# Two transformer blocks on one core: an opening in another order, squares added before TensorE sums them, and sixteen gate vectors moved from the queries' stage to the early experts

## The chip, the cores and the metric

The kernel runs on 1 core of one Trainium2 chip, in a single launch. Its time is the device time of that launch, in microseconds (us). The time of the kernel before is the median of 3 runs.

## What is computed

Two blocks over T = 256 tokens of width D = 2048, in fp32. The first has a forgetting attention beside a gated linear recurrence, and a PEER layer of 16384 experts; the second an S5 state-space mixer with a gated linear unit and a native sparse attention. What matters here, of the first block:

```python
mod = sc @ w_ada[l] + b_ada[l]                      # sc = silu(c)
sh1, sc1, ga1, sh2, sc2, ga2 = jnp.split(mod, N_ADA, axis=-1)
h = _rmsnorm(x, g_mix[l]) * (1.0 + sc1[:, None, :]) + sh1[:, None, :]
mix = _hybrid_mixer(h, w_in[l], ...)                # ends in merged @ w_out
x = x + ga1[:, None, :] * mix
h = _rmsnorm(x, g_ffn[l]) * (1.0 + sc2[:, None, :]) + sh2[:, None, :]
x = x + ga2[:, None, :] * _peer(h, peer_w_q[l], peer_k1[l], peer_k2[l], peer_u[l], peer_v[l])
```

`_peer` projects queries, takes the top 16 of 128 keys twice, combines them, takes the top 16 again and a softmax, and sums the chosen experts' rows of `peer_v`, each weighted by the softmax and by gelu(peer_u row . h). The second block has vectors of the same kind from `w_mod2` and a second condition `c2`.

## The kernel before, in words

It is a hand-written program of five instruction streams: TensorE (PE), VectorE (DVE), ScalarE (ACT), GpSimd (POOL) and SyncE (SP). Named semaphores tie them, and `meet` is a barrier of all of them. Activations stand transposed, 128 features on the partitions and 256 tokens beside, so D is KT = 16 chunks.

**Weights** come in tiles of 1 MB (128x2048 fp32) into `ring`, which has four slots. SP issues their loads in the written order (`load`, L407): tile `pos` waits until slot `pos % 4` is free, so a slot returned late holds up every later load on that queue. `STAGES` gives each stage's tiles for one pass of its loop, the passes, and how many of the tiles are for TensorE and how many are vectors. The stages run in this order: shift_scale, heads, w_out, topk (the PEER queries), tail, hots, early, peer, turn, ssm, glu, ssm_out, kv, nsa, w_o.

**Vectors.** One chunk of a modulation vector is the row sums of a tile of `w_ada` or `w_mod2` times `cond` = silu(c), in two halves. `whole_vec` (L1486 to L1490) does it on DVE in two custom operations and returns the tile's slot. In topk another pair does it for the chunks 80 to 95, which gate the PEER output and aren't read before its end: POOL multiplies the tile by `cond` in place (`vec_times`, L2203), ACT sums it (`vec_sum`). `take_mod` moves finished sums into `mod`.

**Opening.** SP loads four modulation tiles, x, and then tiles and three first `w_in` tiles by turns; ACT's queue loads `cond`, then `vec` (gains and biases). DVE makes 32 vectors, works out the norm's factor rstd once six pairs are done (`norm_rstd`), and writes the normed rows of H as pairs of vectors become ready (L1578). TensorE makes the three first products of head 0 from `head_vec`, chunk by chunk with H. Beside each head's eight ring tiles, three vector tiles go into `head_vec` (`head_beside`) and DVE sums them at L1636.

**Norms.** ACT squares x in pieces (`PIECES`: chunks 0-4, 4-8, 8-12, 12-15, 15-16), and TensorE sums the 16 square tiles with a matrix of ones: `norm_sums` (L600), and `merged_sums` (L608) for two norms over half the width each.

**topk and tail.** Each of 8 heads is two query products (`gemm`, L520), eight score matmuls of the head before (L748) around half a hidden product, and that product's other half. DVE copies the scores (L1739) and picks the best keys; the equality tests against `iota_t` are at L1760. Tail is eight more hidden products, five of them before the transposes of the picked (L763), then `meet`, then three. **Hots** goes on with 16 products; beside them TensorE spreads the weights over a dense block (L780) and ACT copies that (`copy_tokens`). `early_hidden` stores gelu values.

**Early experts.** 32 tiles of peer_v in four groups g of eight tiles j, in two halves. ACT makes a tile's high half `vhi` (L1228), DVE the rest `vlo` (L1804), TensorE multiplies them by the weights' own parts Ghi and Glo (L583, L584, L590) into four banks, and DVE adds each bank to the rows y (`add_rows`, L1812) one group later, at even j. POOL clears y (L2216, `y_clear`). DVE makes the weights of the next group between (`early_weigh`, `early_low`; L1818, L1823). **peer** runs the remaining experts in the same manner, with its own vector tiles (`vbuf`).

## Time and profile before

| | us |
|---|---|
| Median of 3 runs | 3670.26 (3666.49 to 3670.36) |
| The profiled execution | 3664.94 |
| Its span, first to last instruction | 3663.2 |
| Mean granted clock of TensorE | 0.975 |

The span lies 1.7 us under the profiled execution's own time. Times in the trace count from the span's start. On every row the first number is the start, the second the duration; a group of equal instructions is one row with their count, and its duration runs from the first start to the last end, so matmuls that overlap are counted once. What stands in square brackets is the engine's idle time before the row, and what ended it.

### The profile page before, as it was taken

To read this page: it belongs to the slowest core of one execution; us is meant where nothing else is said; L and a number is where in the kernel's file an instruction comes from. 1 tells how busy PE (TensorE), PEld (TensorE's weight loads), DVE (VectorE), ACT (ScalarE), POOL (GpSimd) and SP (SyncE) were. 2 spreads that over 40 slices of the span, in tenths; PEclk is the share of its full clock that TensorE was granted. 3 is DMA by queue.
4 is the path that set the end of the run, shared out by engine and by line. 5 is a ranking of instruction groups with operands and counts; after the bars stand their busy time and mean duration, and the time that the engine had idled before them with its cause. 6 is when DMAs were issued, how large, how long until landed. Compare 5 with 4: busy or idle time off the path is not lost. (4 is left out here: it accounts for less than half of the span.)

```text
span 3663.2 us, 56553 instructions
## 1 busy us (share of the span) xinstructions
PE 3460.7 (94%) x20712; PEld 3063.9 (84%) x20712; DVE 2454.7 (67%) x4494; ACT 1339.0 (37%) x2000; POOL 387.9 (11%) x405
## 2 busy tenths in 40 slices
PE   3799998889989999999999999899999899999998
PEld 2688887779977999999999998577779898999998
DVE  7666556877367777777777776888834634666664
ACT  1232312212234444444444444211112434555553
POOL 0000113410000000000000000577710000000000
PEclk7899998989999999999999999899999999999999
DMA  9678744555765888888888886122246643555543
GB/s 394 267 297 304 257 167 182 202 179 201 263 234 207 297 296 298 295 296 300 298 288 295 297 296 234 58 92 92 92 151 228 247 150 130 188 188 186 184 173 127
DMA packets 123316, 817.72 MB, mean 223 GB/s; under 512 B 12848, under 2 KB 18224, under 8 KB 27184
## 3 DMA queue, kind: packets, MB, share of 16 engines
q1 hardware_dynamic: 105552, 760.26, 57.4%
q10 hardware_dynamic: 17632, 55.63, 4.0%
q8 instruction: 91, 1.49, 0.2%
q14 instruction: 41, 0.34, 0.0%
HBM read 791.65 MB, written 24.18 MB: 223 GB/s over the span
## 5 line engine op out<-in xcount | busy, mean ns | idle before, releaser
L520 PE MATMUL bank<-H,ring 128*128 128x256 f32 x3744 | 849.4, 386 | 39.6 <-ACT H L1064 17.5
L520 PEld LDWEIGHTS bank<-H,ring 128*128 128x128 f32 x3744 | 715.4, 193 | 161.3 <-issue 58.2
L1804 DVE TENSOR_TENSOR vlo<-ring,vhi 128x1024 fp32r<-128x1024 f32 x448 | 548.2, 1225 | 308.1 <-ACT vhi L1228 294.5
L1228 ACT ACTIVATE vhi<-ring 128x1024 fp32r<-128x1024 f32 x448 | 474.8, 1060 | 627.8 <-PE bank L590 350.0
L556 PE MATMUL bank<-Hhi,whi 128*128 128x256 f32 x1920 | 484.0, 290 | 21.1 <-DVE Hlo L1511 10.2
L1500 DVE TENSOR_TENSOR wlo<-ring,whi 128x1024 fp32r<-128x1024 f32 x240 | 292.8, 1227 | 308.3 <-ACT whi L1035 305.1
L557 PE MATMUL bank<-Hlo,whi 128*128 128x256 f32 x1920 | 474.2, 285 | 0.0
L584 PE MATMUL bank<-vhi,Glo 128*128 128x512 f32 x1024 | 400.6, 391 | 0.0
L583 PE MATMUL bank<-vhi,Ghi 128*128 128x512 f32 x1024 | 400.6, 391 | 0.0
L556 PEld LDWEIGHTS bank<-Hhi,whi 128*128 128x128 f32 x1920 | 370.3, 193 | 31.5 <-issue 17.7
L535 PE MATMUL bank<-Fhi,vhi 128*128 128x256 f32 x1536 | 373.0, 280 | 0.0
L536 PE MATMUL bank<-Flo,vhi 128*128 128x256 f32 x1536 | 372.9, 283 | 0.0
L557 PEld LDWEIGHTS bank<-Hlo,whi 128*128 128x128 f32 x1920 | 371.4, 193 | 0.0
L1035 ACT ACTIVATE whi<-ring 128x1024 fp32r<-128x1024 f32 x240 | 253.9, 1059 | 312.3 <-PE bank L561 294.1
L536 PEld LDWEIGHTS bank<-Flo,vhi 128*128 128x128 f32 x1536 | 290.4, 189 | 0.5
L535 PEld LDWEIGHTS bank<-Fhi,vhi 128*128 128x128 f32 x1536 | 288.5, 188 | 0.5
L590 PE MATMUL bank<-vlo,Ghi 128*128 128x512 f32 x1024 | 276.5, 392 | 12.7 <-DVE vlo L1804 12.7
L561 PE MATMUL bank<-Hhi,wlo 128*128 128x256 f32 x1920 | 271.3, 285 | 0.0
L561 PEld LDWEIGHTS bank<-Hhi,wlo 128*128 128x128 f32 x1920 | 249.8, 194 | 0.0
L590 PEld LDWEIGHTS bank<-vlo,Ghi 128*128 128x128 f32 x1024 | 192.3, 188 | 56.1 <-DVE vlo L1804 16.0
L1881 DVE CUSTOM_DVE_ANT_0 arena<-arena,cond 128x1024 f32<-128x1024 f32 x192 | 234.0, 1219 | 0.0
L583 PEld LDWEIGHTS bank<-vhi,Ghi 128*128 128x128 f32 x1024 | 192.7, 188 | 41.4 <-issue 0.9
(412 smaller groups left out, 4489.1 us busy)
## 6 DMA issues: line engine op xcount, KB each, us to landing
ring<-in_peer_u SPq DMA_DIRECT2D x128, 1024.0 KB, 5.5
ring<-in_peer_v SPq DMA_DIRECT2D x128, 1024.0 KB, 5.1
arena<-in_w_mod SPq DMA_DIRECT2D x96, 1024.0 KB, 7.3
ring<-in_w_ada SPq DMA_DIRECT2D x72, 1024.0 KB, 6.4
ring<-in_w_qz SPq DMA_DIRECT2D x64, 1024.0 KB, 4.8
ring<-in_w_in SPq DMA_DIRECT2D x37, 1024.0 KB, 6.0
ring<-in_w_mod SPq DMA_DIRECT2D x32, 1024.0 KB, 5.0
ring<-in_ssm_in SPq DMA_DIRECT2D x32, 1024.0 KB, 5.1
```

The costliest lines, as they stand in the source:

```text
L520: last = mm(out, ring[:, pos % R, k, :], rhs[:, k, :], start=(k == 0), stop=(k == KT - 1))
L535: mm(out, u_hi[:, k, :], Fhi[:, kk, :], start=(kk == 0), stop=False)
L536: mm(out, u_hi[:, k, :], Flo[:, kk, :], start=False, stop=False)
L556: mm(out, whi[:, half, k, :], Hhi[:, kk, :], start=(kk == 0), stop=False)
L557: mm(out, whi[:, half, k, :], Hlo[:, kk, :], start=False, stop=False)
L561: last = mm(out, wlo[:, half, k, :], Hhi[:, kk, :], start=False, stop=(kk == KT - 1))
L583: mm(pair[th][:], G_hi[part][:, n, tok], vhi[:, half, k, :], start=(n == 0), stop=False)
L584: mm(pair[th][:], G_lo[part][:, n, tok], vhi[:, half, k, :], start=False, stop=False)
L590: last = mm(pair[th][:], G_hi[part][:, n, tok], vlo[:, half, k, :], start=False, stop=(n == 7))
L1228: A(vhi[:, half], v_half(pos, half), ACT.Copy).then_inc(s("vhi_ready"), 1)
L1500: v.tensor_tensor(wlo[:, half], ring[:, pos % R, 8 * half:8 * half + 8, :], whi[:, half].bitcast(F32), ALU.subtract).then_inc(s("wlo_ready ...
L1804: v.tensor_tensor(vlo[:, half], v_half(pos, half), vhi[:, half].bitcast(F32), ALU.subtract)\
```

## The change

- **Opening.** `cond` is the first load on SP's queue; eight modulation tiles stand before x; five first `w_in` tiles in place of three, in `scratch`; TensorE reads two more of head 0's products from there. DVE waits for `vec` only at m == 7, where the norm's factor and the first rows stand too. The three loads beside head 0 come after the wait for `f_in_psum`, behind all of head 0's tiles, and DVE's sums of them after the attention's probabilities.
- **Norms' squares.** POOL adds square tiles in pairs (`add_squares`, and a loop of 12 adds for the merged norms); TensorE sums 6 tiles in place of 16, and 4 in place of 16 for the merged. The final norm of the first block stays as it was.
- **Gate vectors.** The tiles 80 to 95 of `w_ada` leave topk, whose loop has 12 tiles in place of 20, and go to early, four in each group, on DVE. Early's four `w_mod2` tiles move into peer's numbering, and four of peer's go to glu, which has 8 vectors in place of 4. The load and Silu of the second condition move from behind the tail to early's last group.
- **Tail and hots.** Seven tail products stand before the transposes and one after the barrier. In hots the product comes before the spread on TensorE, and `early_hidden` before `copy_tokens` on ACT.
- **y.** DVE's wait for the clearing of y moves from before the early loop to before the first `add_rows`.

```diff
-STAGES = dict(shift_scale=(4, 8, 4, 2), heads=(8, HEADS, 5, 3), w_out=(8, 2, 8, 0), topk=(20, 2, 12, 0),
-              tail=(8, 1, 8, 0), hots=(16, 1, 16, 0), early=(36, 1, 32, 4), peer=(16, 12, 16, 0),
-              ssm=(4, 8, 4, 0), glu=(20, 1, 16, 4), ssm_out=(24, 1, 16, 8), kv=(8, 3, 8, 0),
+STAGES = dict(shift_scale=(4, 8, 4, 2), heads=(8, HEADS, 5, 3), w_out=(8, 2, 8, 0), topk=(12, 2, 12, 0),
+              tail=(8, 1, 8, 0), hots=(16, 1, 16, 0), early=(48, 1, 32, 16), peer=(16, 12, 16, 0),
+              ssm=(4, 8, 4, 0), glu=(24, 1, 16, 8), ssm_out=(24, 1, 16, 8), kv=(8, 3, 8, 0),
...
+EARLY_VEC = [(0, 2, 4, 6)] * 3 + [(0, 1, 2, 3)]
...
-            if k == 3:
-                out.append(("w_mod2", g))
+            if k in EARLY_VEC[g]:
+                out.append(("w_ada", 80 + 4 * g + EARLY_VEC[g].index(k)))
...
-GLU_M = [4, 9, 14, 19]
-GLU_W = [pos for pos in range(20) if pos not in GLU_M]
+GLU_M = list(range(2, 24, 3))
+GLU_W = [pos for pos in range(24) if pos not in GLU_M]
...
-FIRST = (0, 1, 4)
+FIRST = (0, 1, 4, 3, 6)
...
-        first_w = head_vec[:].rearrange("p n (k m) -> p n k m", k=KT)
+        first_w = scratch[:, 0:5 * D].rearrange("p (n k m) -> p n k m", n=5, k=KT)
...
+            def first_load(n):
+                sp.dma_start(first_w[:, n], a["w_in"][HEAD_W.index(FIRST[n])]).then_inc(first_loaded[max(n - 2, 0)], 16)
...
+            sp.dma_start(cond[:], a["c"].broadcast_to([P, D])).then_inc(s("cond_loaded"), 16)
             mod_tiles(0, first=True)
+            mod_tiles(1)
             sp.dma_start(x[:], a["x"]).then_inc(x_loaded, 16)
-            for n, pos in enumerate(FIRST):
-                mod_tiles(n + 1)
-                sp.dma_start(first_w[:, n], a["w_in"][HEAD_W.index(pos)]).then_inc(first_loaded[n], 16)
-            with sp.Fori(4, 8) as i:
+            for n in range(4):
+                mod_tiles(n + 2)
+                first_load(n)
+            with sp.Fori(6, 8) as i:
                 mod_tiles(i)
+            first_load(4)
             sp.dma_start(gate_w, a["gate_w"][0]).then_inc(s("gatew_loaded"), 16)
...
-                if pos == 2:
-                    sp.wait_ge(s("f_in_psum"), 1)
-                if pos in (2, 5, 7):
-                    head_beside(0, HEAD_M.index(pos))
+            sp.wait_ge(s("f_in_psum"), 1)
+            for n in range(3):
+                head_beside(0, n)
...
-                        load("topk", i, 5 * h + k, a["w_q"][8 * i + 2 * h + k])
-                    for k in range(2):
-                        load("topk", i, 5 * h + 2 + k, a["w_ada"][80 + 8 * i + 2 * h + k])
-                    load("topk", i, 5 * h + 4, a["peer_u"][4 * i + h])
+                        load("topk", i, 3 * h + k, a["w_q"][8 * i + 2 * h + k])
+                    load("topk", i, 3 * h + 2, a["peer_u"][4 * i + h])
...
-                        sp.dma_start(vbuf[:, n % 2], a["w_mod2"][4 + 8 * i + n].rearrange("p k n -> p (k n)"))\
+                        sp.dma_start(vbuf[:, n % 2], a["w_mod2"][8 * i + n].rearrange("p k n -> p (k n)"))\
...
+            def added_sums(n, name):
+                pe.wait_ge(s("squares_added"), n + 2)
+                for t in range(2):
+                    mm(WA[:, 0:T], ones[:, 0:P], SQ[:, t, :], start=(t == 0), stop=False)
+                for p in (3, 4):
+                    pe.wait_ge(s("squares_ready"), SQUARES[name] + p + 1)
+                    for t in range(*PIECES[p]):
+                        last = mm(WA[:, 0:T], ones[:, 0:P], SQ[:, t, :], start=False, stop=(t == KT - 1))
+                last.then_inc(s("sums_ready"), 1)
...
-                for h in range(HEADS):
-                    for g in range(2):
-                        pe.wait_ge(s("squares_ready"), SQUARES["merged"] + 2 * h + g + 1)
-                        last = mm((WA, WB)[g][:, 0:T], ones[:, 0:P], SQ[:, HEADS * g + h, :], start=(h == 0), stop=(h == HEADS - 1))
+                pe.wait_ge(s("squares_added"), 1)
+                for g in range(2):
+                    mm((WA, WB)[g][:, 0:T], ones[:, 0:P], SQ[:, HEADS * g, :], start=True, stop=False)
+                for g in range(2):
+                    pe.wait_ge(s("squares_ready"), SQUARES["merged"] + 2 * (HEADS - 1) + g + 1)
+                    last = mm((WA, WB)[g][:, 0:T], ones[:, 0:P], SQ[:, HEADS * g + HEADS - 1, :], start=False, stop=True)
...
-            for n, b in enumerate((2, 0, 1)):
+            for b in (2, 0, 1):
                 pe.wait_ge(bank_free[b], 1)
-                pe.wait_ge(first_loaded[n], 16)
+            pe.wait_ge(first_loaded[0], 48)
...
-            gemm("heads", 0, 3, banks[0][:, T:2 * T], 0)
+            def first_product(n, out, lo, hi):
+                for k in range(lo, hi):
+                    last = mm(out, first_w[:, n, k, :], H[:, k, :], start=(k == 0), stop=(k == KT - 1))
+                return last
+            pe.wait_ge(first_loaded[1], 16)
+            first_product(3, banks[0][:, T:2 * T], 0, KT).then_inc(slot_free[3], 1)
             head_gates(0)
-            gemm("heads", 0, 6, banks[3][:, 0:T], 3, 0, halves=(0,))
+            pe.wait_ge(bank_free[3], 1)
+            pe.wait_ge(first_loaded[2], 16)
+            first_product(4, banks[3][:, 0:T], 0, 8)
             head_scores(0)
-            gemm("heads", 0, 6, banks[3][:, 0:T], 3, halves=(1,))
+            pe.wait_ge(slot_free[2], use_of("heads", 0, 6))
+            first_product(4, banks[3][:, 0:T], 8, KT).then_inc(slot_free[2], 1)
...
-            norm_sums("ffn")
+            added_sums(0, "ffn")
...
-                    gemm("topk", i, 5 * h + 4, banks[b][:, 0:T], b, uses[b] + 2 * i + h // 2, halves=(0,))
+                    gemm("topk", i, 3 * h + 2, banks[b][:, 0:T], b, uses[b] + 2 * i + h // 2, halves=(0,))
...
-            for pos in range(5):
+            for pos in range(7):
...
-            for pos in range(5, 8):
-                tail(pos)
+            tail(7)
...
+                gemm("hots", 0, c, banks[c % 4][:, 0:T], c % 4, uses[c % 4] + c // 4)
                 for u in range(3 * c, min(3 * c + 3, 32)):
                     spread_tokens(u)
-                gemm("hots", 0, c, banks[c % 4][:, 0:T], c % 4, uses[c % 4] + c // 4)
...
-            def vec_sum(i, pos, n, col, half):
-                act.wait_ge(s("prod_ready"), 2 * (8 * i + n) + half + 1)
-                w = ring[:, pos % R, 8 * half:8 * half + 8, :].rearrange("p k n -> p (k n)")
-                A(w, w, ACT.Copy, accum_out=mod_ab[:, half, bass.ds(col, 1)])
-                if half == 1:
-                    act.drain().then_inc(slot_free[pos % R], 1)
...
-            act.dma_start(cond[:], a["c"].broadcast_to([P, D])).then_inc(s("cond_loaded"), 16)
...
-                    for k in range(2):
-                        for half in range(2):
-                            vec_sum(i, 5 * h + 2 + k, 2 * h + k, 80 + 8 * i + 2 * h + k, half)
...
+            for pos in range(5, 7):
+                early_hidden("tail", 0, pos, 8 + pos, pos % 4, 2 + pos // 4, pos % 4)
...
-            act.dma_start(cond[:], a["c2"].broadcast_to([P, D])).then_inc(s("cond_loaded"), 16)
             act.sem_inc(s("spread_copied"), 3)
-            act.wait_ge(s("cond_loaded"), 32)
-            A(cond[:], cond[:], ACT.Silu).then_inc(s("cond_ready"), 1)
-            for pos in range(5, 8):
-                early_hidden("tail", 0, pos, 8 + pos, pos % 4, 2 + pos // 4, pos % 4)
+            early_hidden("tail", 0, 7, 15, 3, 3, 3)
...
-                for m in range(6 * c, min(6 * c + 6, 64)):
-                    copy_tokens(m)
...
+                for m in range(6 * c, min(6 * c + 6, 64)):
+                    copy_tokens(m)
...
+                    if g == 3 and j == 5:
+                        product(act, "early", 0, AT["early", "w_ada", 95])
+                        act.dma_start(cond[:], a["c2"].broadcast_to([P, D])).then_inc(s("cond_loaded"), 16)
+                    if g == 3 and j == 7:
+                        act.wait_ge(s("cond_loaded"), 32)
+                        A(cond[:], cond[:], ACT.Silu).then_inc(s("cond_ready"), 1)
...
-            dve.wait_ge(vec_in, 16)
             for m in range(KT):
                 for k in range(2):
                     whole_vec("shift_scale", m // 2, 2 * (m % 2) + k, m + KT * k)
-                if m == 5:
+                if m == 7:
+                    dve.wait_ge(vec_in, 16)
                     norm_rstd("mix", D)
...
-            with dve.Fori(0, HEADS) as i:
+            def vectors(i):
...
+            def head(i, first=False):
...
+                if not first:
+                    vectors(i)
...
+                if first:
+                    vectors(i)
...
+            head(0, first=True)
+            with dve.Fori(1, HEADS) as i:
+                head(i)
...
-            take_mod(80, 96)
-            dve.wait_ge(s("cond_ready"), 2)
...
-            dve.wait_ge(s("y_clear"), 1)
...
+                        if g == 0 and j == 2:
+                            dve.wait_ge(s("y_clear"), 1)
                         add_rows(16 * g, j // 2 - 1)
-                    if j == 4:
-                        whole_vec("early", 0, AT["early", "w_mod2", g], 96 + g)
+                    if j - 1 in EARLY_VEC[g]:
+                        n = 80 + 4 * g + EARLY_VEC[g].index(j - 1)
+                        whole_vec("early", 0, AT["early", "w_ada", n], n)
...
+            take_mod(80, 96)
...
+            dve.wait_ge(s("cond_ready"), 2)
...
-                v.tensor_copy(mod_ab[:, :, bass.ds(100 + 8 * i, 8)], peer_sums)
+                v.tensor_copy(mod_ab[:, :, bass.ds(96 + 8 * i, 8)], peer_sums)
...
-                if g % 4 == 3:
-                    whole_vec("glu", 0, GLU_M[g // 4], 196 + g // 4)
+                if g % 2 == 1:
+                    whole_vec("glu", 0, GLU_M[g // 2], 192 + g // 2)
...
+            for i in range(1, HEADS - 1):
+                for g in range(2):
+                    pool.wait_ge(s("squares_ready"), SQUARES["merged"] + 2 * i + g + 1)
+                    tt(SQ[:, HEADS * g, :], SQ[:, HEADS * g, :], SQ[:, HEADS * g + i, :], ALU.add)
+                pool.drain()
+            pool.drain().then_inc(s("squares_added"), 1)
+            def add_squares(name):
+                for p in range(3):
+                    pool.wait_ge(s("squares_ready"), SQUARES[name] + p + 1)
+                    tt(SQ[:, 4 * p:4 * p + 2, :], SQ[:, 4 * p:4 * p + 2, :], SQ[:, 4 * p + 2:4 * p + 4, :], ALU.add)
+                    pool.drain()
+                    if p:
+                        tt(SQ[:, 0:2, :], SQ[:, 0:2, :], SQ[:, 4 * p:4 * p + 2, :], ALU.add)
+                        pool.drain()
+                pool.drain().then_inc(s("squares_added"), 1)
...
+            add_squares("ffn")
...
-                w = ring[:, pos % R, 8 * half:8 * half + 8, :].rearrange("p k n -> p (k n)")
-                gp.tensor_tensor(w, w, cond[:, D // 2 * half:D // 2 * half + D // 2], ALU.mult)\
-                    .then_inc(s("prod_ready"), 1)
...
```

The first loads on SP's queue, before. `cond` isn't among them, since ACT's queue loads it; `head_vec` holds the first `w_in` tiles.

```order
L407 DMA ring<-in_w_ada 128x2048 x4
L434 DMA x<-in_x 128x4096
L407 DMA ring<-in_w_ada 128x2048 x4
L437 DMA head_vec<-in_w_in 128x2048
L407 DMA ring<-in_w_ada 128x2048 x4
```

And in the change:

```order
L439 DMA cond<-in_c 128x2048
L410 DMA ring<-in_w_ada 128x2048 x8
L442 DMA x<-in_x 128x4096
L410 DMA ring<-in_w_ada 128x2048 x4
L437 DMA scratch<-in_w_in 128x2048
L410 DMA ring<-in_w_ada 128x2048 x4
```

`cond` has come in front, and x stands four modulation tiles further back.

TensorE at the tail, before: the products of 16 matmuls each, the transposes of the picked (into work_a, b, c), and the first of hots.

```order
L520 MATMUL bank<-H,ring 128x256 x80
L763 MATMUL work_a<-ident,arena 128x128 x2
L763 MATMUL work_b<-ident,arena 128x128 x2
L763 MATMUL work_c<-ident,arena 128x128 x2
L520 MATMUL bank<-H,ring 128x256 x48
L780 MATMUL work_a<-hotB,hotA 128x128 x4
```

And in the change:

```order
L526 MATMUL bank<-H,ring 128x256 x112
L791 MATMUL work_a<-ident,arena 128x128 x2
L791 MATMUL work_b<-ident,arena 128x128 x2
L791 MATMUL work_c<-ident,arena 128x128 x2
L526 MATMUL bank<-H,ring 128x256 x32
L807 MATMUL work_a<-hotB,hotA 128x128 x4
```

Two products of 16 matmuls have moved ahead of the transposes; behind them stand one of the tail and the first of hots.

SP's queue in early, before:

```order
L407 DMA ring<-in_peer_u 128x2048 x24
L407 DMA ring<-in_peer_v 128x2048 x4
L407 DMA ring<-in_w_mod 128x2048
L407 DMA ring<-in_peer_v 128x2048 x8
L407 DMA ring<-in_w_mod 128x2048
L407 DMA ring<-in_peer_v 128x2048 x8
```

And in the change:

```order
L410 DMA ring<-in_peer_u 128x2048 x24
L410 DMA ring<-in_peer_v 128x2048
L410 DMA ring<-in_w_ada 128x2048
L410 DMA ring<-in_peer_v 128x2048 x2
L410 DMA ring<-in_w_ada 128x2048
L410 DMA ring<-in_peer_v 128x2048 x2
L410 DMA ring<-in_w_ada 128x2048
```

Every third tile is now a vector's, where it was every ninth; the last group has its four by turns with single peer_v tiles.

## Rows read from the trace of the kernel before

**Rows 1.** The page's line on each engine: busy us, share of the span, instructions.
```profile
PE 3460.7 (94%) x20712; PEld 3063.9 (84%) x20712; DVE 2454.7 (67%) x4494; ACT 1339.0 (37%) x2000; POOL 387.9 (11%) x405
```

**Rows 2.** TensorE's waits: engine, line, waited for: us in total, times, longest.
```profile
PE work_a L748 <- DVE arena L1739: 18.2, 4, 8.8
...
PE bank L590 <- DVE vlo L1804: 12.7, 7, 8.7
```

**Rows 3.** The opening as a window: us, PE, PEld, DVE, ACT, POOL, clock, DMA share, GB/s.
```profile
12.00:60.00 48.00, 9.36 (x33) 7.68 (x34) 41.26 (x83) 11.24 (x17) 0.00 (x0) 0.76 1.01 422
```

**Rows 4.** Timeline, opening and head 0: start, us, engine, line, operation, count [idle before <-releaser].
```profile
14.28 1.22 DVE L1486 CUSTOM_DVE_ANT_0 ring<-ring,cond 128x1024 f32<-128x1024 f32 x1 [12.92 <-DMA vec<-in_vec]
...
111.86 0.48 DVE L1578 SCALAR_TENSOR_TENSOR arena<-x,gain,rstd 128x256 f32<-128x256 f32 x1
...
122.47 8.80 PE L520 MATMUL bank<-H,ring 128*128 128x256 f32 x32 [7.18 <-DMA ring<-in_w_in]
...
139.85 1.22 DVE L1636 CUSTOM_DVE_ANT_0 head_vec<-head_vec,cond 128x1024 f32<-128x1024 f32 x1 [7.07 <-DMA head_vec<-in_w_ada]
...
150.04 22.40 PE L520 MATMUL bank<-H,ring 128*128 128x256 f32 x96
```

**Rows 5.** Timeline, TensorE, the merged norm's sums and w_out.
```profile
428.51 0.70 PE L608 MATMUL work_a<-arena,ones 128*128 128x256 f32 x2 [1.01 <-ACT arena L1129]
...
435.52 110.67 PE L726 MATMUL bank<-arena,ring 128*128 128x256 f32 x512
```

**Rows 6.** Timeline, sums of the ffn and the last norm, with their last squares.
```profile
546.02 7.07 PE L600 MATMUL work_a<-arena,ones 128*128 128x256 f32 x32
...
548.14 0.42 ACT L1046 ACTIVATE arena<-x 128x256 f32<-128x256 f32 x1 [5.98 <-DVE x L1680]
...
3642.49 7.07 PE L600 MATMUL work_a<-arena,ones 128*128 128x256 f32 x32
...
3643.21 0.42 ACT L1046 ACTIVATE arena<-x 128x256 f32<-128x256 f32 x1 [2.60 <-DVE x L2008]
```

**Rows 7.** Timeline, GpSimd and VectorE in the queries' stage.
```profile
599.08 9.48 POOL L2203 TENSOR_TENSOR ring<-ring,cond 128x1024 f32<-128x1024 f32 x4 [36.43 <-DMA ring<-in_w_ada]
...
603.93 4.91 DVE L1760 TENSOR_TENSOR arena<-arena,iota_t 128x256 f32<-128x256 f32 x2
...
765.90 0.69 DVE L1739 COPY arena<-work_a 128x512 f32<-128x512 f32 x1 [0.51 <-issue]
...
774.59 0.76 DVE L1760 TENSOR_TENSOR arena<-arena,iota_t 128x256 f32<-128x256 f32 x2
...
788.28 0.69 DVE L1739 COPY arena<-work_a 128x512 f32<-128x512 f32 x1 [0.51 <-issue]
```

**Rows 8.** Timeline, TensorE, two heads of the queries' stage and the tail.
```profile
591.70 20.89 PE L520 MATMUL bank<-H,ring 128*128 128x256 f32 x96
...
613.31 20.89 PE L520 MATMUL bank<-H,ring 128*128 128x256 f32 x96
...
813.04 0.69 PE L763 MATMUL work_a<-ident,arena 128*128 128x128 f32 x2 [7.04 <-DVEq L1784]
...
815.62 22.49 PE L520 MATMUL bank<-H,ring 128*128 128x256 f32 x96 [1.05 <-ACTq L368]
```

**Rows 9.** Timeline, early experts: y's memset, and TensorE's passes with the low halves.
```profile
1011.51 3.51 POOL L2216 MEMSET y<- 128x4096 f32 x1 [252.43 <-DMA early_hidden<-y]
...
1016.38 2.08 PE L590 MATMUL bank<-vlo,Ghi 128*128 128x512 f32 x4 [8.75 <-DVE vlo L1804]
...
1046.46 1.20 PE L590 MATMUL bank<-vlo,Ghi 128*128 128x512 f32 x4 [0.73 <-DVE vlo L1804]
...
1049.31 1.07 PE L590 MATMUL bank<-vlo,Ghi 128*128 128x512 f32 x4
...
1052.03 1.07 PE L590 MATMUL bank<-vlo,Ghi 128*128 128x512 f32 x4
```

**Rows 10.** Loads of ring tiles by SyncE from 1020 to 1070 us, summary.
```profile
DMA to landing us min/median/max: 4.7/4.8/7.7
```

More of the change, by code:

```diff
@@ L487, in _ @@
                     load("ssm", i, 2 * t + 1, a["ssm_in"][KT + 2 * i + t])
-            for pos in range(20):
-                load("glu", 0, pos, a["w_mod2"][100 + GLU_M.index(pos)] if pos in GLU_M else a["w_glu"][GLU_W.index(pos)])
+            for pos in range(24):
+                load("glu", 0, pos, a["w_mod2"][96 + GLU_M.index(pos)] if pos in GLU_M else a["w_glu"][GLU_W.index(pos)])
             for pos in range(24):
@@ L750, in _ @@
                     last.then_inc(s("s_in_psum"), 1)
-                    gemm("topk", i, 5 * h + 4, banks[b][:, 0:T], b, halves=(1,))
+                    gemm("topk", i, 3 * h + 2, banks[b][:, 0:T], b, halves=(1,))
             for b in range(4):
@@ L1011, in _ @@
                 uses[b] += 4
-            norm_sums("final2")
+            added_sums(2, "final2")
             meet(pe, met)
@@ L1615, in _ @@
             conv_w = V("conv_w").rearrange("p (a b) -> p a b", b=4)
-            with dve.Fori(0, HEADS) as i:
+            def vectors(i):
+                for n in range(3):
+                    dve.wait_ge(head_loaded[n], 16 * (i + 1))
+                    for half in range(2):
+                        w = head_vec[:, n, D // 2 * half:D // 2 * half + D // 2]
+                        ins = v.tensor_tensor_reduce(w, w, cond[:, D // 2 * half:D // 2 * half + D // 2], 1.0, 0.0,
+                                                     ALU.mult, ALU.add, accum_out=head_sums[:, half, n:n + 1])
+                    ins.then_inc(head_free[n], 1)
+                dve.drain()
+                v.tensor_copy(mod_ab[:, :, bass.ds(56 + 3 * i, 3)], head_sums[:])
+            def head(i, first=False):
                 v.tensor_scalar(cm[:, 0, :], fl[:, 5, :], ident[0:8, bass.ds(i, 1)], None, ALU.mult)
@@ L2271, in _ @@
             meet(pool, met)
+            add_squares("final2")
             meet(pool, met)
```

36 lines of the change are left out of this document (10 added, 26 removed).

## The prediction, made before the changed kernel ran

> **What bounds the kernel now.** I read the page's engine line first, then TensorE's waits, then the timeline around each place that the change touches. The engine line [rows 1]: TensorE (PE) is busy 94% of the span, VectorE (DVE) 67%. So time can only come from PE's gaps, or from work taken off PE. PE's waits [rows 2] name two gaps that the edits aim at: 18.2 us in four waits for DVE's copy of the queries' scores (L1739), and 12.7 us in seven waits for the low halves of peer_v (L1804), 8.7 of it once. The other targets are the opening, where PE has next to nothing to do, and the norms' sums. 0.2% of the time, 7.3 us, is about what this measurement tells from no change.
>
> **Opening and head 0.** In the window from 12 to 60 us [rows 3] PE is busy 9.36 of 48 us, DVE 41.26, and the DMA engines are full (share 1.01, 422 GB/s, so 1 MB takes about 2.49 us). DVE's first vector op starts at 14.28 [rows 4], after 12.92 us for `vec`. Now `cond` is first on the SP queue and the wait for `vec` moves behind vector 16: I put the start at about 8. But `cond`, 16 modulation tiles, x (2 MB) and one first tile, 20 MB, land by 3 + 20 x 2.49 = 53, so the vectors then wait for DMA, and DVE's sixteenth ends at 55 to 56, not earlier for its early start. From there DVE is the bound as before: the norm's rstd and eight rows, moved here, about 7.5; 16 tiles of some 2.6 (two 1.22 us ops [rows 4] and what reads them out), 41; the other rows, 5. The last row of H, at 111.86 before [rows 4], comes at about 110: 2 us earlier. What goes as well is head 0's wait for its weight tile (7.18) and the cold product behind it (8.80 for one of about 7) [rows 4], since its two products now sit in scratch. The loads of head 0's three vectors, on which DVE waited 7.07 to 139.85 [rows 4], move behind `f_in_psum` on the SP queue, and head 1's weights stand behind them: head 0's attention, with PE busy on nothing else, ends some 12 us earlier, at 138, while head 1's three first tiles land at about 140, 150 (its slot waits for DVE's vector) and 157. Before, head 1's product began at 150.04 [rows 4]; its third tile is then about 8 earlier than before. Bounds: 2 + 1 for the earlier row alone, and the whole 12 less one for the rest. I take 8, **-8 (-11 to -3)**.
>
> **Norms' squares.** Before, the merged norm's sums run from 428.51 to 435.52 as 16 matmuls [rows 5]. Now POOL has added heads 1 to 6 while the heads ran, and 4 matmuls of 0.44 are left: 1.8 in place of 7.0, **-5.2**. For the ffn norm, 16 matmuls take 7.07 from 546.02, to 553.09; the last square ends at 548.56 [rows 6]. With 6 matmuls the sum ends about 0.5 behind that square, 549.1: **-4.0**. For final2, 3642.49 + 7.07 = 3649.56, the last square 3643.63 [rows 6]; POOL's last add, of a piece squared earlier, and the last two matmuls end at about 3645.2: -4.4, and l1 is built alike: **-8.8** for both. POOL's adds cost about 1.2 us each (half of the 128x1024 one of 9.48 / 4 us [rows 7]), five a norm, beside PE's last products.
>
> **Queries' stage.** In the four heads with the longest waits, POOL multiplies gate vectors (9.48 us for four [rows 7]) and the DVE pair at L1760 takes 4.91; with POOL silent the same pair takes 0.76 [rows 7]. The 32 POOL ops go, so all heads should run like the undisturbed ones: DVE's copies of two such heads start at 765.90 and 788.28, 22.38 apart [rows 7]. PE's head is 613.31 - 591.70 = 21.61 long [rows 8]. The waits of 18.2 us [rows 2] go; DVE then falls 0.8 us a head behind, which PE's next scores don't notice within eight heads. On the clock of before: DVE's first copy at about 592, its eighth at 592 + 7 x 22.38 = 748.6, and the picked some 24.8 later (a head and the softmax), at 773, in place of 813.04. PE's eighth scores begin at 613.31 + 6 x 21.61 - 0.9 = 742.1; they, a half product (3.45) and seven tail products of 6.91 (a third of 20.89 [rows 8]) fill it to 794.8. The picked are there first, so the 7.04 us wait before the transposes [rows 8] goes. The transposes, copies and barrier keep 2.6 (813.04 to 815.62), the last product takes 6.9: hots begin at 804.3, before at 815.62 + 22.49 = 838.11 [rows 8]. **-33.8**: 18.2 and 7.0 are the waits, the other 8 the slower PE behind each (22.49 in place of 20.89 for 96 matmuls [rows 8], three such groups, and scores). Were only the waits worth something, it would be -25, the lower end. In the tail ACT's early_hidden has two more products before the barrier; they hide.
>
> **The wait for y's clearing.** The memset of y starts at 1011.51, released by the store of early hidden values, takes 3.51, and DVE waited for it before the first low half: PE stalls 8.75 us to 1016.38 and its next pass is cold, 2.08 for one of 1.07 [rows 9]. The wait now stands before the first add_rows, two tiles (10.9 us) later. PE starts at 1007.6, but ACT waits for the same store until 1011.5 and makes the second tile's high half only then; about 2 is given back. **-8 (-10 to -4.5)**: if the memset held DVE's lows for its 3.51 us, as POOL's multiplications held L1760, it would be -4.5. The Trainium skill (SBUF — State Buffer, Who interferes with whom) says that a DVE instruction with two SBUF inputs contends with a GpSimd instruction that reads SBUF, and not with one that only writes it, as a memset. By that rule the sum is -54.3, by L1760's rows taken over to the memset -50.8; no row here shows the two side by side.
>
> **Early experts.** 12 tiles more: 16 vectors in place of 4. A PE half takes 2.72 us (1049.31 to 1052.03 [rows 9]), a tile 5.44, its weights 4.8 from issue to landing [rows 10]. DVE has the 2.4 us for a vector in an odd tile, where it has no rows to add. But the ring has four slots, and a vector's slot goes back only behind DVE's turn in the next tile. So the peer_v tile that follows in that slot is issued late; ACT's high half is wanted about 2.5 us before PE's product, and I get 0.6 to 0.75 us of stall a vector for 12 of them (0.73 follows the vector before 1046.46 now [rows 9]), 8; the last group has four vectors in a row, 6; a group's loads by ACT beside them 2. The six stalls of before, 12.7 - 8.7 = 4.0 [rows 2], are in these: -4. **+12 (+5 to +20)**. The four shifted w_mod2 vectors in peer take the place of others, glu gets four more beside DVE idle time: 0, the cover being 5 us a pair; if it were gone, 2.6 each.
>
> **Small.** In hots the product goes before the spread, the store of early hidden values lands about 1 later; `cond`'s Silu sits beside the last early tile. **+1.5**.
>
> **Sum.** -8 - 5.2 - 4.0 - 8.8 - 33.8 - 8 + 12 + 1.5 = -54.3. From the profiled execution's 3664.94 that is 3611; it lies 5.3 below the median 3670.26, to which the sum is carried over: 3670.3 - 54.3 = 3616. I say **3615**. Bounds of the terms added as squares: (5, 9, 3.5, 8) give about 13.
>
> **Rivals.**
> - Early vectors hidden as DVE's idle time would allow (for: 1.1 us idle between lows; against: slot order above): +12 becomes 0, **3604**. 12%.
> - DVE's slow pairs aren't POOL's doing, so the queries' stage still has PE waiting (for: the overlap could be coincidence; against: 4.91 and 0.76 split exactly so). Then only tail order is left, -8.8: **3641**. 6%.
> - The opening gains nothing, since head 1's tiles come when they came (for: they queue behind the moved loads): **3623**. 6%.
> - POOL's adds read SBUF while DVE makes low halves for the last products, each side holding the other as at L1760. Five adds of about 1.2 in each of two norms, all exposed, is 12: **3628**. 5%. The Trainium skill's rule on the shared port (SBUF — State Buffer, Who interferes with whom) says that they would, this time against the change; the trace agrees in L1760's 4.91 us, but shows no POOL add beside a low.
> - The change doesn't do what it says in the tail (picked later than PE's seventh product): up to 7 lost, **3622**. 2%.
> - **Slower**: each of 16 gate tiles in early exposes its whole landing, since ring order makes each peer_v tile wait for a vector's slot. 16 x 4.8 [rows 10] = 77 in place of 12: **3681**. It decides from (54.3 + 12) / 16 = 4.1 us a vector on. For: in order ring, DVE's turn late. Against: three other slots are full, 4 us of slack. 3%.
> - The forecast as it stands: 66%.
>
> **How the numbers follow.** The predicted time is that of the forecast, 3615. Its own range is 13 either way, 3602 to 3628. The hidden case widens it to 3600; of the upper ones 3641 lies apart, and reaching to 3637 takes in the forecast's bounds with the opening's and adds' cases together. Left out: 3641 and 3681, and the ends, under 2 in 10. Faster by over 0.2% (under 3663) in all cases but the slower: 0.95; within: 0.02; slower: 0.03.
>
> **What would show it.** DVE's first vector op at about 8 and head 1's product at about 140; merged sums 4 matmuls; the L1760 pair 0.76 in every head and no PE waits over 1 us for the scores; hots' start near 804; PE's stall for the lows gone at the first early product and about a dozen of 0.6 us between; the sums before w_out, l1 and final2 short. The prediction is wrong if early shows PE stalls of over 2 us a vector, if L1760 stays at several us, or if the sums' PE time is bought with longer DVE lows before them.

## The result, and the profile after

The changed kernel takes 3616.72 us (median of 4 runs, 3616.24 to 3626.62), beside 3668.38 (4 runs, 3663.80 to 3670.36) for the kernel before: a ratio of 0.9868, with a 95% interval from 0.9852 to 0.9883. The profiled executions are 48.7 us apart (3664.94 and 3616.24), the medians 51.7. The forecast was 54.3 less, 3615.

Where it went, from the first rows of each stage on TensorE in the two traces, and in the last column the terms of the forecast:

| Up to the first product or sum of | before, us | after, us | gained in all | gained here | forecast here |
|---|---|---|---|---|---|
| the merged norm | 428.51 | 423.77 | 4.7 | 4.7 | 8 |
| w_out | 435.52 | 425.60 | 9.9 | 5.2 | 5.2 |
| the queries' stage | 570.62 | 550.81 | 19.8 | 9.9 | 4.0 |
| hots | 838.11 | 783.25 | 54.9 | 35.1 | 33.8 |
| early | 1005.44 | 950.84 | 54.6 | -0.3 | -1.5 |
| peer | 1199.38 | 1157.11 | 42.3 | -12.3 | -4 (8 - 12) |
| ssm's glu | 2680.57 | 2638.62 | 42.0 | -0.3 | 0 |
| kv, behind l1's norm | 2903.16 | 2858.68 | 44.5 | 2.5 | 4.4 |
| the end of the span | 3663.2 | 3614.5 | 48.7 | 4.2 | 4.4 |

Two numbers of the table are worked out: hots begins 22.49 us behind 815.62 before, and one tail product of 6.91 us behind 776.34 after. In the rows a product has 32 matmul records, so x64 is two products.

The engine line of the page after, which answers to [rows 1], and below it TensorE's waits, which answer to [rows 2] (engine, line, waited for: us in total, times, longest):

```profile
span 3614.5 us, 56289 instructions
...
PE 3435.4 (95%) x20628; PEld 3038.4 (84%) x20628; DVE 2457.7 (68%) x4574; ACT 1337.0 (37%) x1960; POOL 354.0 (10%) x400
```

```profile
PE bank L589 <- ACT vhi L1241: 15.2, 9, 3.6
...
PE bank L526 <- ACT H L1083: 11.4, 1, 11.4
...
PE bank L596 <- DVE vlo L1833: 5.1, 6, 1.8
```

The waits for the scores (18.2 us) are gone from the list. In early, the wait for the low halves has shrunk from 12.7 to 5.1, and a new one stands above it: 15.2 us in nine waits for ScalarE's high halves, which weren't waited for at all before.

**The opening**, rows of the timeline after (start, us, engine, line, operation, count [idle before <-releaser]), which answer to [rows 4]:

```profile
9.05 1.23 DVE L1505 CUSTOM_DVE_ANT_0 ring<-ring,cond 128x1024 f32<-128x1024 f32 x1 [7.71 <-DMA ring<-in_w_ada]
...
34.02 1.23 DVE L1505 CUSTOM_DVE_ANT_0 ring<-ring,cond 128x1024 f32<-128x1024 f32 x1 [4.21 <-DMA ring<-in_w_ada]
...
111.75 0.48 DVE L1597 SCALAR_TENSOR_TENSOR arena<-x,gain,rstd 128x256 f32<-128x256 f32 x1
...
116.41 7.17 PE L716 MATMUL bank<-H,scratch 128*128 128x256 f32 x32
...
143.77 16.59 PE L526 MATMUL bank<-H,ring 128*128 128x256 f32 x64 [4.07 <-DMA ring<-in_w_in]
```

VectorE starts 5.2 us earlier and loses it again to DMA behind x. The last row of H stands at 111.75, in place of 111.86: nothing was gained up to there. The gain is in the warm product of 7.17 us, without a wait ahead of it, and it ends in a new wait of 4.07 for head 1's weights.

**ffn norm and the queries' stage.** First VectorE before, with the three operations ahead of the norm that the forecast had left out; then after, the first of these three (the other two take 0.18 as well) and the places that answer to [rows 7, 8]:

```profile
553.50 2.28 DVE L1546 TENSOR_TENSOR mod_ab<-mod_ab,vec 128x24 f32<-128x24 f32 x1
555.86 2.21 DVE L1536 TENSOR_SCALAR gain<-mod_ab 128x16 f32<-128x16 f32 x1
558.15 2.22 DVE L1538 TENSOR_TENSOR gain<-gain,vec 128x16 f32<-128x16 f32 x1
```

```profile
539.79 0.18 DVE L1565 TENSOR_TENSOR mod_ab<-mod_ab,vec 128x24 f32<-128x24 f32 x1
...
550.81 19.62 PE L526 MATMUL bank<-H,ring 128*128 128x256 f32 x80 [11.43 <-ACT H L1083]
...
580.05 0.76 DVE L1791 TENSOR_TENSOR arena<-arena,iota_t 128x256 f32<-128x256 f32 x2
...
763.24 0.42 DVE L1808 TENSOR_REDUCE arena<-arena 128x16 f32<-128x256 f32 x1 [11.03 <-ACT arena L1202]
...
774.25 0.38 PE L791 MATMUL work_a<-ident,arena 128*128 128x128 f32 x2
...
776.34 14.08 PE L526 MATMUL bank<-H,ring 128*128 128x256 f32 x64 [1.27 <-ACTq L371]
```

Operations on 16 or 24 elements took 2.2 us each, beside GpSimd's first three multiplications of 2.34 us (from 553.41 on); without them 0.18. That is 6.1 us, and the idle time ahead of the queries falls from 17.53 to 11.43 by just that. In the tail the picked keys are ready at 764.6, 9.7 us ahead of the transposes.

**Early**, after; it answers to [rows 9], and the last line, the summary of the ring's loads from 960 to 1150 us, to [rows 10]:

```profile
958.82 3.52 POOL L2255 MEMSET y<- 128x4096 f32 x1 [430.46 <-DMA early_hidden<-y]
...
960.26 2.36 DVE L1833 TENSOR_TENSOR vlo<-ring,vhi 128x1024 fp32r<-128x1024 f32 x2 [6.50 <-ACT vhi L1241]
...
960.28 0.50 PE L589 MATMUL bank<-vhi,Ghi 128*128 128x512 f32 x1 [3.62 <-ACT vhi L1241]
...
974.02 2.00 ACT L1241 ACTIVATE vhi<-ring 128x1024 fp32r<-128x1024 f32 x2 [3.21 <-DMA ring<-in_peer_v]
```

```profile
DMA to landing us min/median/max: 4.7/6.4/9.8
```

Two low halves take 2.36 us in the middle of the memset, as they do elsewhere: the memset doesn't hold VectorE. The row at 974.02 shows what the new vectors cost: ScalarE waits for a peer_v tile.

### The profile page after: what moved, and what is told of

Same layout as the page of the kernel before. It is cut to its first block and busy times, and to the rows that moved or that the text cites. A ratio compares the mean times of both kernels' runs of the same rounds, so it can differ in the third digit from the quotient of the medians.

```text
span 3614.5 us, 56289 instructions
## 1 busy us (share of the span) xinstructions
PE 3435.4 (95%) x20628; PEld 3038.4 (84%) x20628; DVE 2457.7 (68%) x4574; ACT 1337.0 (37%) x1960; POOL 354.0 (10%) x400
## 5 line engine op out<-in xcount | busy, mean ns | idle before, releaser
L526 PE MATMUL bank<-H,ring 128*128 128x256 f32 x3680 | 828.8, 384 | 30.3 <-PEq L371 13.4
L526 PEld LDWEIGHTS bank<-H,ring 128*128 128x128 f32 x3680 | 696.9, 192 | 149.8 <-issue 51.3
L589 PE MATMUL bank<-vhi,Ghi 128*128 128x512 f32 x1024 | 402.0, 393 | 15.2 <-ACT vhi L1241 15.2
L1505 DVE CUSTOM_DVE_ANT_0 ring<-ring,cond 128x1024 f32<-128x1024 f32 x208 | 253.6, 1256 | 18.0 <-DMA ring<-in_w_ada 14.1
```

What stands on the lines that cost most here:

```text
L526: last = mm(out, ring[:, pos % R, k, :], rhs[:, k, :], start=(k == 0), stop=(k == KT - 1))
L589: mm(pair[th][:], G_hi[part][:, n, tok], vhi[:, half, k, :], start=(n == 0), stop=False)
```

## The experiments

All but the last two are one run with a profile each, so they are read by stages in their traces. The kernel before took 3667.14 and 3667.11 us beside the first eight.

**GpSimd's multiplications alone.** In the kernel before, GpSimd only passes the semaphore on, and ScalarE copies a column in place of the sum:

```diff
-                gp.tensor_tensor(w, w, cond[:, D // 2 * half:D // 2 * half + D // 2], ALU.mult)\
-                    .then_inc(s("prod_ready"), 1)
+                pool.sem_inc(s("prod_ready"), 1)
...
-                A(w, w, ACT.Copy, accum_out=mod_ab[:, half, bass.ds(col, 1)])
+                A(mod_ab[:, half, bass.ds(col, 1)], w[:, 0:1], ACT.Copy)
```

> The kernel before, with GpSimd's 32 multiplications and the real sums on ScalarE left out (ScalarE copies one column in their place): chunks 80 to 95 of the modulation are wrong, while their tiles still come through the ring in the old order. Theory (GpSimd's multiplications hold VectorE's operations): the four waits for the scores, 18.2 us before, fall under 2; the idle time ahead of the queries' first product falls from 17.5 to 11.4; the L1760 pair is 0.76 in every head; all in all 30 to 38 us less than before, 3627 to 3635. Rival (the vector tiles in the ring, or their place in ScalarE's order, are the cause): the waits stay, and the time stays within 6 us of before.

Measured 3631.32, 35.8 less than before. TensorE's waits in its trace:

```profile
PE bank L520 <- ACT H L1064: 11.5, 1, 11.5
...
PE work_a L763 <- DVEq L1784: 4.0, 1, 4.0
```

The four waits for the scores are gone, the wait ahead of the queries is 11.5 in place of 17.5, and that at the tail 4.0 in place of 7.0. The stage from the queries' first product to the first spread takes 239.1 us (565.17 to 804.26), before 267.3. The tiles still came through the ring, in the old order, and ScalarE still took its turn at each, so the rival falls. ScalarE's real sums were left out together with GpSimd's multiplications, and this run alone doesn't split the two. The trace of before does: 8 of L1760's 32 operations there take 2.42 or 2.57 us in place of 0.42, all 8 lie over a GpSimd multiplication and none over a ScalarE sum, while two that lie over a ScalarE sum take 0.42 and 0.43. So it was GpSimd's work that held VectorE.

**TensorE sums 16 squares again.** The changed kernel with `added_sums` turned back into `norm_sums`, `merged_sums` as before, and GpSimd's adds left out:

```diff
-            added_sums(1, "l1")
+            norm_sums("l1")
...
-            add_squares("l1")
```

> The changed kernel without GpSimd's adds: TensorE sums 16 squares again in the merged, ffn, l1 and last norm. Theory (the gain is TensorE's matmuls, and the adds cost nothing): +5.2 +3.8 +4.4 +4.4 = 18 us, 3634. Rival (the adds hold VectorE's low halves in ssm_out and w_o, as the small gain of 2.5 us at l1 suggests): these products run 2 us or more faster without them, and the kernel takes at most 3632.

Measured 3642.18, 25.5 above the changed kernel. 9 us of that aren't the sums': its ssm stage runs in a longer rhythm (see the last section), 10.3 us longer, of which the glu gives back 1.2. Without them it is 16.5, under the 18 expected, and both theories hold a part. From ssm_out's first product to l1's sums it takes 92.9 us (2769.36 to 2862.25), before 92.9 as well, and with the adds 94.7 (2751.69 to 2846.34). VectorE in that stage, of the changed kernel and without the adds:

```profile
2806.54 3.62 POOL L2203 TENSOR_TENSOR arena<-arena 128x512 f32<-128x512 f32 x2 [21.66 <-ACT arena L1065]
...
2807.09 1.92 DVE L1505 CUSTOM_DVE_ANT_0 ring<-ring,cond 128x1024 f32<-128x1024 f32 x1
2808.94 2.30 DVE L1505 CUSTOM_DVE_ANT_0 ring<-ring,cond 128x1024 f32<-128x1024 f32 x1
```

```profile
2813.24 1.22 DVE L1503 CUSTOM_DVE_ANT_0 ring<-ring,cond 128x1024 f32<-128x1024 f32 x1
```

The adds hold a vector's two operations, 0.7 and 1.1 us beyond their 1.22. Behind each of the two vectors that this happens to, TensorE waits 0.6 us for a low half (at 2812.72 and 2836.64), which it doesn't without the adds. They cost the stage 1.8 of the 4.3 that they save TensorE there. In w_o, which has no vectors, they hold low halves of the weights, two of them, at 3561.97 and 3585.01; a low half elsewhere takes 1.23:

```profile
3561.97 1.96 DVE L1519 TENSOR_TENSOR wlo<-ring,whi 128x1024 fp32r<-128x1024 f32 x1 [1.32 <-ACT whi L1054]
```

No wait of TensorE follows, and the stage loses nothing: from w_o's first product to the final norm's sums 94.3 us with the adds, 95.5 without, 94.8 before.

**The wait for y's clearing, back in its old place:**

```diff
+            dve.wait_ge(s("y_clear"), 1)
             for g in range(4):
...
-                        if g == 0 and j == 2:
-                            dve.wait_ge(s("y_clear"), 1)
```

> The changed kernel with VectorE's wait for the clearing of y back in front of the early loop. Theory (the wait was on the path for the part of the 8.7 us that ScalarE's own wait doesn't cover): TensorE idle 8 to 9 us at the first low half in place of 3.6, the kernel 4 to 6 us slower, about 3621. Rival (ScalarE's wait for the same store bounds the stage anyway): no change, 3616.

Measured 3627.33; from early's first product to peer's it takes 216.1 us in place of 206.3, so the move is worth 9.9, more than either theory had. TensorE's row:

```profile
963.13 2.07 PE L596 MATMUL bank<-vlo,Ghi 128*128 128x512 f32 x4 [9.26 <-DVE vlo L1833]
```

The wait is 9.26 in place of 3.62. The other 4 us lie behind it: the granted clock is 0.75 from 963 to 975 us, where the changed kernel has 0.87 from 960 to 973, and the next wait for ScalarE is 3.38 in place of 2.02.

**Early's sums left out**, their tiles and places kept:

```diff
-                        whole_vec("early", 0, AT["early", "w_ada", n], n)
+                        loaded(dve, "early", 0, AT["early", "w_ada", n])
+                        v.tensor_copy(mod_ab[:, :, n:n + 1], ring[:, AT["early", "w_ada", n] % R, 0:2, 0:1])
+                        dve.drain().then_inc(slot_free[AT["early", "w_ada", n] % R], 1)
```

> The changed kernel, with VectorE's 32 sums of early's gate tiles left out (one small copy each; chunks 80 to 95 are wrong), tiles and places as they are, so that a slot comes back about 2.5 us earlier. Theory (late slots behind VectorE's sums make the peer_v tiles late): the early stage, 206 us from its first product to peer's first, falls to 196 to 199, and the kernel to about 3608. Rival (the 12 more tiles on SyncE's queue and the loads themselves cost it): the stage stays at 203 or more.

Measured 3614.10, with the 9 us of the longer ssm rhythm in it. Early takes 195.2 us, from 949.43 to peer's first product:

```profile
1144.64 0.39 PE L541 MATMUL bank<-Fhi,vhi 128*128 128x256 f32 x1 [1.15 <-ACT vhi L1241]
```

That is 11.1 less than 206.3, slightly more than the theory's 7 to 10, and the rival's 203 or more is refuted. TensorE's waits of over 0.3 us, up to that row's, fall from 20.8 to 14.3 us in all. The run shortens VectorE's work and the time that a slot is held together; it doesn't say which of the two counts. The next one does.

**The gate tiles behind the odd tiles, summed in the same turn:**

```diff
-EARLY_VEC = [(0, 2, 4, 6)] * 3 + [(0, 1, 2, 3)]
+EARLY_VEC = [(1, 3, 5, 7)] * 3 + [(0, 1, 2, 3)]
...
-                    if j - 1 in EARLY_VEC[g]:
+                    k = j if g < 3 else j - 1
+                    if k in EARLY_VEC[g]:
```

> The changed kernel with early's gate tiles of the groups 0 to 2 behind the odd tiles of peer_v, and summed in the same turn of VectorE in which they arrive, in place of behind the even ones and a turn later: a vector's slot comes back about one peer_v tile sooner after its load, with the same VectorE work and the same loads. Theory (late slots and the pairs of loads that are issued together behind them make peer_v late): the median time from issue to landing falls from 6.4 us to near 5, and the early stage, 206.3 us, is 3 to 8 shorter. Rival (VectorE's time a turn is what counts): 0 to 1 us of change; or the vector waits for its tile and the stage grows.

Measured 3605.88. Early takes 195.8 us (950.78 to 1146.59), 10.5 less than 206.3, with the same loads and the same sums. That is nearly all that leaving out the sums gave. The summary of the ring's loads in it, as above:

```profile
DMA to landing us min/median/max: 4.7/5.6/10.6
```

The slot is held for a shorter time: the stage bears the theory out, by more than the 3 to 8 expected, and the rival that VectorE's time counts falls. The median landing fell only to 5.6, not near 5. In a second version with this edit (below) early took 200.1 us, so there only 6.2 of the 10.5 came back.

**All gate tiles in w_out.** One behind each w_out tile (`w_out=(16, 2, 8, 8)`, `early=(32, 1, 32, 0)`, w_out's products at 2 * g, and on VectorE):

```diff
                 merged_residual(g)
+                if g < 15:
+                    whole_vec("w_out", g // 8, 2 * (g % 8) + 1, 80 + g)
```

> The changed kernel with all 16 gate tiles in w_out, one behind each w_out tile, and none in early. It measures the whole price of the 16 tiles in early. Forecast: early shrinks from 206.3 to 185 to 189 us, since its PE halves of 2.72 us make 174 for 64, and two stalls for ScalarE stay; w_out's 110.7 us grow by 0 to 3, because VectorE has 4 us free a tile there and two tiles land in the 6.9 us of one product. About 3600. Rival (GpSimd's operations and VectorE's discretisation steps in w_out hold the vectors, their slots come back late, and the w_out tiles behind them on SyncE's queue too): w_out 8 us or more longer.

Measured 3612.09. Early takes 187.5 us (966.37 to 1153.85), so the 16 tiles cost it **18.8**, of which 7.7 stayed when only their sums were left out (195.2). But from w_out's first product to the queries' it takes 140.5 in place of 125.2: w_out is longer by more than the rival's 8, and 15.3 of the 18.8 go back. TensorE's waits name 8.8 of it, for late w_out tiles; and beside GpSimd's operations four of the vectors' take 2.05 to 2.9 us there in place of 1.22:

```profile
PE bank L755 <- DMA ring<-in_w_out: 8.8, 6, 2.5
```

**Head 0's loads and sums in another order.** The three loads stand behind the wait for `f_in_psum`, but ahead of tiles 6 and 7; VectorE sums them at the end of head 0:

```diff
-            sp.wait_ge(s("f_in_psum"), 1)
-            for n in range(3):
-                head_beside(0, n)
...
+                if pos == 5:
+                    sp.wait_ge(s("f_in_psum"), 1)
+                    for n in range(3):
+                        head_beside(0, n)
...
-                if first:
-                    vectors(i)
                 whole_vec("heads", i, 5, 33 + 3 * i)
...
                 whole_vec("heads", i, 7, 34 + 3 * i)
+                if first:
+                    vectors(i)
```

> The changed kernel with the three loads beside head 0 issued right behind f_in_psum, ahead of the waits for the slots of the tiles 6 and 7, and head 0's three sums at the end of its turn on VectorE, behind the vectors of the ring tiles 5 and 7. Theory (head 1 waits for its weights, which stand behind these loads, and for slots that VectorE returns late): head 1's product starts at 140 in place of 143.8, and w_out's first 4 to 8 us earlier. Rival (a later head's VectorE work then bounds): under 1 us at w_out's first product.

Measured 3609.80. Head 1's product starts at 139.78, without a wait:

```profile
139.78 13.98 PE L527 MATMUL bank<-H,ring 128*128 128x256 f32 x64
```

The merged sums start 5.3 us earlier (418.47), and so does w_out's first product, inside the 4 to 8 forecast:

```profile
420.30 29.95 PE L755 MATMUL bank<-arena,ring 128*128 128x256 f32 x138
```

At peer it is 6.7.

**Five tail products ahead of the transposes, three behind:**

```diff
-            for pos in range(7):
+            for pos in range(5):
                 tail(pos)
...
-            tail(7)
+            for pos in range(5, 8):
+                tail(pos)
```

> The changed kernel with five products ahead of the transposes and three behind the barrier, as before. Theory (GpSimd's silence alone brings the picked so early that the order of the tail is worth little): TensorE waits about 4.3 us before the transposes, since the picked come at 764.6 and the fifth product ends at 760.4, and the kernel is 4 to 6 us slower. Rival (the order is worth as much as before, a wait of 7 us and cold products): 9 us or more.

Measured 3622.88; the first spread starts at 798.07 in place of 790.25, 247.1 us behind the queries' first product in place of 239.4. The expected wait is there, and behind it the granted clock is 0.70 from 764 to 780 us, where the changed kernel has 1.00 from 774 to 790: 4 becomes 7.7. The kernel's time is 6.2 us longer, at the end of the 4 to 6 expected and under the rival's 9:

```profile
764.70 0.69 PE L791 MATMUL work_a<-ident,arena 128*128 128x128 f32 x2 [4.04 <-DVEq L1815]
```

**Together, and a version that beats both kernels.** First the same turn and head 0's new order:

> The changed kernel with both edits that shortened a stage by themselves: early's gate tiles behind odd tiles of peer_v (early 10.5 us shorter), and head 0's loads and sums in the new order (6.4 us off the end). They lie in different stages, so they should add: 3616.7 - 10.5 - 6.4 = 3600. If the ssm stage falls into its longer rhythm (389 in place of 379 us) in a run, that run is 10 us above.

Measured 3604.07 (5 runs, 3599.27 to 3614.86). The 3600 was missed by 4: in the profile, early still takes 200.1 us (944.97 to 1145.03) and not 195.8. Its first waits are 4.0 us in place of 1.8 and 1.0, and the granted clock in its first 30 us is 0.94 in place of 1.00, which is part of it; the rest stays open. Then also with the last four gate tiles in the tail (`tail=(12, 1, 8, 4)`, tiles behind the fourth to seventh product):

```diff
+            for n in (0, 1):
+                whole_vec("tail", 0, TAIL_M[n], 92 + n)
             dve.wait_ge(s("vs_exp"), 1)
...
             dve.drain().then_inc(s("picked_ready"), 1)
+            for n in (2, 3):
+                whole_vec("tail", 0, TAIL_M[n], 92 + n)
             meet(dve, met)
```

> The same, with the last four gate tiles out of early's last group and into the tail, where VectorE waits 11 us for the softmax's exponential and 12 us for the barrier: two are summed ahead of each. Forecast: early's last group loses its stalls of 2.0, 1.9 and 2.2 us and the cold passes behind them, 6 to 8 us; the tail stays as it is, since the tiles are loaded behind the fourth to seventh product, and each product's tile still lands before its turn. 3592 to 3594. Rival (a vector's slot in the tail comes back late and holds up the next product's tile): TensorE waits for a tile in the tail, and 0 to 3 us are left.

Measured **3597.39** (5 runs, 3593.30 to 3606.63), a ratio to the kernel before of 0.9816 (0.9801 to 0.9831), against 0.9868 of the changed kernel. The forecast of 3592 to 3594 was missed by 3 to 5. Early takes 191.7 us (945.18 to 1136.89), 8.4 less, and in the tail TensorE has the same single wait as without the tiles:

```profile
770.68 14.08 PE L530 MATMUL bank<-H,ring 128*128 128x256 f32 x64 [1.27 <-ACTq L372]
```

## Why the prediction was right, and where its terms were off

The forecast of 54.3 less came out as 48.7 in the profiles and 51.7 in the medians. The mechanisms hold; single terms were missed by up to 8 us, on both sides, and the closeness of the sum is in part luck: without the 6.1 us that it lacked ahead of the queries, it would have been 11.7 too high.

- **Queries' stage**: -33.8 forecast, -35.1 measured, for the reason given. The experiments split it: 28.2 for GpSimd's silence (239.1 in place of 267.3 us; ScalarE's sums went with it), 7.7 for the tail's order, together 0.8 more than measured. One step was wrong and hidden: "the picked some 24.8 later" left out that VectorE waits 11.0 us there for ScalarE's exponential, which stands behind five hidden products. The picked keys came at 764.6, 11 later than forecast once the 19.8 gained ahead are taken off; TensorE's seventh product was later still.
- **Norms**: the merged norm -5.2 as forecast, the ffn sums -3.8 (4.0), the last norm -4.3 (4.4). At l1 "4.4, built alike" was mis-sized, since 2.5 were left: in ssm_out the adds cost 1.8 ahead of it. This was the rival of the adds, right in its mechanism and for 1.8 of its 12 us. The adds hold operations of VectorE that read two SBUF operands, as the Trainium skill says (SBUF — State Buffer, Who interferes with whom): here the trace agrees, with 1.92 and 2.30 us in place of 1.22 for a vector's two operations, and 1.96 in place of 1.23 for a low half in w_o. The price was paid by the vectors, which the rival didn't have; of its low halves two were held, in w_o, and no wait of TensorE followed.
- **What the sum lacked**: 6.1 us ahead of the queries. I priced GpSimd's operations only where TensorE waited for the scores, and not in the norm's small operations, where the first three of them ran. The rows at 553.50 to 560.37 stood in the trace of before.
- **The opening**: -8 forecast, -4.7 measured. Two steps failed. "2 us earlier" was 0.1: the sixteenth vector ended at 57.3 and not at 55 to 56, with DMA waits of 4.2 and 2.2 ahead. And head 1's first product came at 143.77 instead of 140, since the three loads of head 0 went out only at 128.7, behind the wait for tile 7's slot on SP. With these moved, the product stands at 139.78, and the opening gains 10.0 at the merged sums (4.7 and 5.3 more), past the forecast's 8.
- **y's clearing**: -8 forecast, -9.9 measured by putting the wait back into the changed kernel. What was weighed there came out by the rule of the Trainium skill on the same page: the memset, which only writes, didn't hold the low halves (2.36 us for two).
- **Early**: +12 was forecast for 12 more tiles, and no run measures just these. All 16 cost 18.8 beside none. Beside the kernel before, with the wait for y's clearing where it was, early is 22.2 longer (216.1 in place of 193.9), above the upper bound of 20. The two terms together, y's clearing and early, were forecast at +4 and measured +12.3: this is the largest miss. The step that failed is "its weights 4.8 from issue to landing". The mechanism, slots that come back late, was right: returning them sooner gave 11.1 back without the sums and 10.5 with them. But two peer_v tiles go out behind a vector's slot 0.4 us apart; from 1042 to 1100 us the first of each pair lands after 4.9 to 5.6 us and the second after 7.0 to 7.8, and the median landing is 6.4. So the waits sit mostly with ScalarE, 1.5 to 3.6 us each, and not as 0.6 us ones with VectorE only.
- **Small**: +1.5 forecast, 0.3 found in hots.

The rival "early vectors hidden" is refuted by the 18.8, and so is the slower one: 18.8 over 16 is 1.2 us a vector, not 4.1.

## What to carry to other kernels

Where GpSimd works beside VectorE, look for short VectorE operations with long durations everywhere in the trace, not only where TensorE waits; here GpSimd's silence was worth 28.2 and 6.1 us, for 18.8 paid where its work went. When a tile for another engine goes into a shared ring, ask in which turn its slot comes back and which loads leave together then: the 16 tiles cost 18.8 us as they stood, and 8.3 (195.8 against 187.5) with 12 of them one place later and summed in the same turn; in the second version with that edit it was 12.6. Look also for an engine that waits long for something else: VectorE's 11 and 12 us in the tail took four of the tiles without a new wait of TensorE.

## What the runs showed that I had not expected

The ssm stage has two rhythms. Its time, from its first product to that of the glu, is 378.8 us before, and 378.4 to 379.4 in ten of the twelve profiles; it is 389.3 and 389.1 in the runs without the adds and without early's sums, whose code in this stage is the same as in the others. In these two TensorE waits for VectorE twice in each pass, 0.6 and 1.0 us, from the fourth pass on, and GpSimd waits for VectorE 83 us in all, in place of 35. The first row is TensorE's, in the run without the adds; the second is a group of VectorE's operations over 95 us of that run, and the third the same group over 95 us of the changed kernel, at half the mean duration:

```profile
2465.24 1.13 PE L860 MATMUL work_b<-arena 32*128 32x256 f32 x4 [1.04 <-DVE arena L1999]
```

```profile
L1968 DVE TENSOR_SCALAR var<-iota_t,arena 128x256 f32<-128x256 f32 x8 | 9.1, 1135 | 0.9 <-issue 0.9
```

```profile
L1970 DVE TENSOR_SCALAR var<-iota_t,arena 128x256 f32<-128x256 f32 x10 | 5.4, 542 | 1.2 <-issue 1.2
```

Here VectorE and GpSimd interleave all the time, so it may be that the order in which they meet keeps itself up once it is set: in the two long profiles the stage's third product starts 24.7 and 24.8 us behind its first, in the ten others 26.2 to 26.8, and the long operations begin 95 us into the stage and stay. That is a guess; what sets the rhythm wasn't tried. It could explain why a single run of one kernel lies 10 us above the rest (3626.62 beside three of 3616 to 3617), which has no profile to show it. A difference of 10 us between two single runs says nothing until the ssm stage has been compared.
